# Layer B of a two-layer trunk: the results of the first four pairs of maps turned by VectorE and carried by transfers

## What is computed

```python
a = attn_map(q1b, k1) - lam * attn_map(q2b, k2)          # one pair of maps
o = einsum("bhqk,bhkd->bhqd", a, v)                      # 8 pairs, 128 columns each
o = o * rsqrt(mean(square(o), -1) + SUBLN_EPS)           # the norm of each pair
o = o * b_subln_g[j] * (1.0 - lambda_init)
x = layer_norm(ALPHA * x + o.reshape(B, S, D) @ b_w_o[j], ...)
```

## Time and profile before

| | |
|---|---|
| median of 3 runs | 590.24 us |
| the profiled execution | 590.63 us, of which its span 588.8 us |
| TensorE (PE) busy | 578.4 us, 98% of the span |
| VectorE (DVE) busy | 450.8 us, 77% |
| ScalarE (ACT) busy | 333.2 us, 57% |
| GpSimd (POOL) busy | 50.8 us, 9% |
| layer B's mixer, last 60 us of it | 340 to 400 us of the span |

### The profile page before, as it was taken

How to read it: one execution, slowest core, us unless ns; L and a number is a source line. 1 busy time by engine, 2 the same in 40 slices (tenths; PEclk the granted TensorE clock), 3 DMA queues, 4 the chain that set the end, 5 groups by cost and what they waited for, 6 DMA issues and landing times.

```text
span 588.8 us, 7729 instructions
## 1 busy us (share of the span) xinstructions
PE 578.4 (98%) x2708; PEld 473.0 (80%) x2708; DVE 450.8 (77%) x820; ACT 333.2 (57%) x557; POOL 50.8 (9%) x84
## 2 busy tenths in 40 slices
PE   8999999999999999999999999999999999999995
PEld 6887877888888888888888888888888888888884
DVE  4889996976688768767879796778677887766656
ACT  4767673345566656554545678945455565555530
POOL 5300000400000000000120003132000000000003
PEclk9999999999999999999999999999999999999998
DMA  8897876556768797866366965342965889767511
GB/s 302 296 325 227 277 220 173 195 181 206 223 205 267 251 350 231 261 235 202 143 212 216 300 183 173 132 144 72 314 186 178 254 260 339 247 228 244 179 36 71
DMA packets 96242, 128.65 MB, mean 218 GB/s; under 512 B 13468, under 2 KB 74188, under 8 KB 96204
## 3 DMA queue, kind: packets, MB, share of 16 engines
q1 hardware_dynamic: 94764, 123.97, 66.1%
q0 software_dynamic: 1152, 4.19, 2.0%
q10 hardware_dynamic: 288, 0.00, 0.0%
HBM read 108.23 MB, written 1.05 MB: 186 GB/s over the span
## 4 chain that ended last, share of the span: by engine, by line
PE 94%; DVE 2%; DMA 1%; SPq 1%; ACT 0%; issue 0%; DVEq 0%
PE wide L1305 17%; PE wide L1307 17%; PE wide L1306 17%; PE score L1307 6%; PE score L1306 6%; PE score L1305 6%; PE outb L1307 3%; PE turn L1307 3%; PE outb L1306 3%; PE turn L1306 3%; PE turn L1305 3%; PE outb L1305 3%; PE score L1321 1%; DMA xs<-in_x 1%; DMA spare<-turned 1%; PE wide L1400 1%
## 5 line engine op out<-in xcount | busy, mean ns | idle before, releaser
L988 DVE TENSOR_TENSOR w_lo<-raw,w_hi 128x2048 fp32r<-128x2048 f32 (+1 forms) x120 | 210.6, 1776 | 60.3 <-ACT w_hi L794 60.2
L794 ACT ACTIVATE w_hi<-raw 128x2048 fp32r<-128x2048 f32 (+1 forms) x126 | 184.1, 1488 | 101.5 <-PE wide L1307 48.2
L1305 PE MATMUL wide<-w_hi,oT_hi 128*128 128x512 f32 x240 | 94.7, 395 | 0.3 <-DVE oT_lo L1195 0.3
L1307 PE MATMUL wide<-w_hi,oT_lo 128*128 128x512 f32 x240 | 93.5, 390 | 0.0
L1306 PE MATMUL wide<-w_lo,oT_hi 128*128 128x512 f32 x240 | 93.5, 389 | 0.0
L1305 PE MATMUL wide<-w_hi,xT 128*128 128x512 f32 x224 | 89.7, 401 | 0.5 <-DVE xT L1013 0.3
L1307 PE MATMUL wide<-w_hi,xT 128*128 128x512 f32 x224 | 87.4, 390 | 0.0
L1306 PE MATMUL wide<-w_lo,xT 128*128 128x512 f32 x224 | 87.3, 390 | 0.0
L1305 PE MATMUL score<-w_hi,xT 128*128 128x512 f32 x160 | 62.2, 389 | 0.0
L1306 PE MATMUL score<-w_lo,xT 128*128 128x512 f32 x160 | 62.2, 389 | 0.0
L1307 PE MATMUL score<-w_hi,xT 128*128 128x512 f32 x160 | 62.2, 389 | 0.0
(11 more groups left out here) (164 smaller groups left out, 835.6 us busy)
## 6 DMA issues: line engine op xcount, KB each, us to landing
raw<-in_ffn_w_in SPq DMA_DIRECT2D x88, 512.0 KB, 5.4
raw<-in_ffn_w_out SPq DMA_DIRECT2D x22, 1024.0 KB, 7.5
kT<-turned SPq DMA_DIRECT2D x104, 128.0 KB, 2.8
raw<-in_a_w_qkv SPq DMA_DIRECT2D x9, 1024.0 KB, 6.9
raw<-in_w_kv_shared SPq DMA_DIRECT2D x8, 1024.0 KB, 5.9
raw<-in_a_w_o SPq DMA_DIRECT2D x4, 1024.0 KB, 6.0
raw<-in_b_w_q SPq DMA_DIRECT2D x4, 1024.0 KB, 5.1
raw<-in_b_w_o SPq DMA_DIRECT2D x4, 1024.0 KB, 5.4
```

What stands on the lines that cost most here:

```text
L794: ins = nc.scalar.activation(w_hi[c % RING][:, part], raw[c % RAW_RING][:, part], ACT.Copy)
L988: ins = nc.vector.tensor_tensor(w_lo[c % RING][:, part], raw[c % RAW_RING][:, part], w_hi[c % RING][:, part].bitcast(F32), ALU.subtract)
L1305: nc.tensor.matmul(dst, a_hi, b_hi, start=start, stop=False, skip_group_check=True)
L1307: return nc.tensor.matmul(dst, a_lo, b_hi, start=False, stop=stop, skip_group_check=True)
```

## The change

For the pairs 0 to 3 (`EARLY = 4`) `outT`, `out_hi` and `out_lo` of each pair are dropped. In their place:
- `out_turn` k (VectorE): one block transpose of `head_out` into the tile `turned`, after `subln` k; `subln` k+1 waits for it instead of for the TensorE transpose.
- `out_move` 0 (SP), once for the four pairs: a wait for the fourth turn, then four transfers of 128 KB from `turned` to `qk_rows`.
- `out_hi` 0 (ScalarE): four activations of 128x256, for all four pairs, from `qk_rows`; `out_lo` 0 (VectorE): eight operations of 128x128. The planner is told that they take 1.6 and 2.3 us, and that `out_hi` 0 comes behind `exp` 13 and `out_lo` 0 behind `norm` 6.
- every `wo` with kt of 0 to 3 needs `out_lo` 0.

`squares`, the scratch output of `square`, gets a second buffer. Pairs 4 to 7 are as before.

```diff
+    "out_turn": ("DVE", 0.45),
+    "out_move": ("SP", 3.0),
...
-LAG = {"move": 3.0, "prob_move": 3.0}
+LAG = {"move": 3.0, "prob_move": 3.0, "out_move": 3.0}
+EARLY = 4
...
-            add(("subln", k), ("mean", k), ("outT", k - 1))
-            add(("outT", k), ("subln", k))
-            add(("out_hi", k), ("outT", k))
-            add(("out_lo", k), ("out_hi", k))
+            add(("subln", k), ("mean", k), ("outT", k - 1), ("out_turn", k - 1))
+            if k < EARLY:
+                add(("out_turn", k), ("subln", k), *[("move", column(mat, 1)) for mat in range(2)])
+            else:
+                add(("outT", k), ("subln", k))
+                add(("out_hi", k), ("outT", k))
+                add(("out_lo", k), ("out_hi", k))
+            if k == EARLY - 1:
+                add(("out_move", 0), ("out_turn", k))
+                add(("out_hi", 0), ("out_move", 0))
+                add(("out_lo", 0), ("out_hi", 0))
+            if k == 6 and m == 13:
+                after[("out_hi", 0)].append(("exp", 13))
+                after[("out_lo", 0)].append(("norm", 6))
...
-                after[("wo", kt, st, half)].append(("out_lo", kt // 2 if A else kt))
+                after[("wo", kt, st, half)].append(("out_lo", kt // 2 if A else kt if kt >= EARLY else 0))
...
+        elif not A and step in (("out_hi", 0), ("out_lo", 0)):
+            takes = {"out_hi": 1.6, "out_lo": 2.3}[step[0]]
...
+            def out_move():
+
+                sp.wait_ge(early_turned_done, EARLY)
+                for a in range(4):
+                    sp.dma_start(early_moved[:, a * EARLY * 64:(a + 1) * EARLY * 64],
+                                 early_turned[32 * a:32 * a + 32].rearrange("p b k s j -> p b (k s j)")).then_inc(early_carried, 16)
...
+                    elif kind == "out_hi" and m < EARLY:
+                        act.wait_ge(early_carried, 64)
+                        for k in range(EARLY):
+                            last = nc.scalar.activation(oT_hi[:, k, :].rearrange("p (s a j) -> p s a j", s=ST, a=4), early_rows(k),
+                                                        ACT.Copy, scale=sub_gain[:, 0:1])
+                        last.then_inc(ohi_done, 1)
...
+                    elif kind == "out_turn":
+                        if m == 0:
+                            for mat in range(2):
+                                dve.wait_ge(moved[mat, 1], 128)
+                        dve.wait_ge(head_done, m + 1)
+                        nc.vector.transpose(early_turned[:, :, m].rearrange("p b s j -> p s b j"),
+                                            head_out.rearrange("p s (i b) -> p s b i", b=4)).then_inc(early_turned_done, 1)
+                    elif kind == "out_lo" and layer == 1 and m < EARLY:
+                        dve.wait_ge(ohi_done, SETS + 1)
+                        for k in range(EARLY):
+                            for st in range(ST):
+                                tokens = slice(st * P, (st + 1) * P)
+                                last = nc.vector.scalar_tensor_tensor(
+                                    oT_lo[:, k, tokens].rearrange("p (a j) -> p a j", a=4), early_rows(k)[:, st],
+                                    sub_gain[:, 0:1], oT_hi[:, k, tokens].bitcast(F32).rearrange("p (a j) -> p a j", a=4),
+                                    ALU.mult, ALU.subtract)
+                        last.then_inc(olo_done, 1)
...
+                            elif kt < EARLY:
+                                pe.wait_ge(olo_done, SETS + 1)
```

More of the change, by code:

```diff
@@ L296, in mixer_schedule @@
             turn_bank_free = None
-        elif step[0] in ("qkT_out", "probT_out") or not A and step[0] == "out_lo":
+        elif step[0] in ("qkT_out", "probT_out") or not A and step[0] == "out_lo" and step[1] >= EARLY:
             turn_bank_free = end[step]
@@ L440, in yoco_trunk @@
         head_out = spare[:, 2 * SEQ:3 * SEQ].rearrange("p (s d) -> p s d", s=ST)
-        squares = spare[:, 3 * SEQ:4 * SEQ].rearrange("p (s d) -> p s d", s=ST)
+        squares = spare[:, 3 * SEQ:5 * SEQ].rearrange("p (n s d) -> p n s d", n=2, s=ST)
         mean_sq = sb("mean_sq", [P, 2, ST])
@@ L454, in yoco_trunk @@
         prob_stage = [prob_stage[n].rearrange("p (b s k q) -> p b s k q", b=4, s=BATCH, k=3) for n in (0, 1, 2, 1)]
+        early_turned = turned[:, :, :, :].rearrange("p n b q -> p (n b q)")[:, 0:EARLY * SEQ].rearrange(
+            "p (b k s j) -> p b k s j", b=4, k=EARLY, s=ST)
+        early_moved = qk_rows[:, 0:EARLY * SEQ]
         conv_rows = sb("conv_rows", [4 * FT, LAYERS, P])
@@ L519, in yoco_trunk @@
         ohi_done, olo_done = sem("ohi_done"), sem("olo_done")
+        early_turned_done, early_carried = sem("early_turned_done"), sem("early_carried")
         y_done, var_done, std_done, norm_x_done = sem("y_done"), sem("var_done"), sem("std_done"), sem("norm_x_done")
@@ L533, in carried, with early_rows @@
             return in_moved.rearrange("p a (j s t) -> p j s a t", j=4, s=ST)[:, part]
+        def early_rows(k):
+            return early_moved.rearrange("p (a k s j) -> p k s a j", a=4, k=EARLY, s=ST)[:, k]
         def by_quarters(tile):
@@ L597, in load @@
                         move(layer, n)
+                    elif kind == "out_move":
+                        out_move()
                     else:
@@ L884, in _ @@
                         for st in range(ST):
-                            last = nc.scalar.activation(squares[:, st, :], head_rows[:, m % 2, st * P:(st + 1) * P],
+                            last = nc.scalar.activation(squares[:, m % 2, st, :], head_rows[:, m % 2, st * P:(st + 1) * P],
                                                         ACT.Square, accum_out=mean_sq[:, m % 2, st:st + 1])
@@ L1185, in _ @@
                         dve.wait_ge(rms_done, m + 1)
-                        if m >= 1:
+                        if m > EARLY:
                             dve.wait_ge(turn_filled, fill_of[(1, "outT", m - 1)] + 1)
+                        elif m:
+                            dve.wait_ge(early_turned_done, m)
                         for st in range(ST):
@@ L1191, in _ @@
                         last.then_inc(head_done, 1)
+                    elif kind == "out_turn":
[15 more added lines that the diff above has]
+                        last.then_inc(olo_done, 1)
                     elif kind == "out_lo":
-                        dve.wait_ge(ohi_done, SETS * layer + m + 1)
+                        dve.wait_ge(ohi_done, m + 1 if layer == 0 else SETS + 2 + m - EARLY)
                         if layer == 0:
```

## The result

The changed kernel has a median of 595.27 us (594.49 to 596.55, 4 runs), the kernel before 590.16 us in the same comparison. The ratio is 1.0088, 95% interval 1.0076 to 1.0101: **5.1 us slower**. I had said 592.6 with a range to 595.1, so the direction was right and the size was half of what came.

What follows compares the result with a forecast made beforehand. TensorE, busy 98% of the span, was taken as the bound. The profiled 590.63 us, less 0.9 for transposes, plus 3.3 idle, gave 593.0, or 592.6 for the median (+2.4); range 590.3 to 595.1.

Steps and rivals of the forecast that it cites:

- The gain: TensorE, four pairs of transposes removed: 0.225 us a pair by the starts, 0.9 us saved in all.
- The rival of dearer transposes: TensorE: the removed transposes save 2.2 us instead of 0.9, giving 591.3 us; chance 0.03.
- The mechanism: TensorE idles about 3.3 us before the first `wo`, nothing behind gives it back; `pv_out` 4, not the transfer, is late.
- Step 1: VectorE: `norm` 4 goes ahead of `subln` 3, put at 367.3; `out_turn` 3 takes 0.45 us and ends at 368.3.
- Step 2: `out_move` on SP: last issue at 370.3, landing 2.7 us after issue at 373.0, at worst 376.8.
- Step 3: ScalarE: `out_hi` 0 stands behind `drain` (5, 1), `exp` 14 and `pv_out` 4, which ends at 374.7, later than the transfer by 1.7.
- Steps 4 and 5: `out_hi` 0 on ScalarE takes 1.5 us, `out_lo` 0 on VectorE 1.95; `wo` starts at about 378.3.
- step 6: TensorE from 372.6 to 378.3: 5.7 us with 2.34 us of other work, so about 3.3 us idle.
- The clock: TensorE in the gap, busy 2.3 of 5.7 us: clock stays 1.00; its fall shared a rival's chance of 0.10.
- My rival of a late landing or a lower clock: Transfers meet the norm rows, or TensorE's clock falls: +4 to +6, 594.2 to 596.2 us; chance 0.10.
- The rival that ended on the other side, hidden: At the first `wo`, TensorE has enough other work until the rows are split: 589.3 to 590.2 us; chance 0.08.

Runs made afterwards that it cites:

- e4: The kernel before, with the two transposes of each of the eight pairs made four times: 595.45 us, 5.29 above the kernel before.
- e8: The changed kernel without the four transfers, `out_hi` 0 and `out_lo` 0 reading `turned` directly: 595.79 us, ratio 1.0095.
- e1: The changed kernel with a planner rule that puts the split of chunk 64 behind `out_hi` 0 and `out_lo` 0: 593.79 us, ratio 1.0065.
- e2: The changed kernel, its order kept, with 17 matmuls whose result nobody reads put into TensorE's gap: 594.11 us, ratio 1.0063.
- e3: The changed kernel with chunk 64's split behind `out_hi` 0 and `out_lo` 0, and 13 unread matmuls in TensorE's gap: 592.79 us, ratio 1.0046.
- e7: The change in two sets of two pairs, in the kernel before's order with urgent VectorE steps moved ahead and `out_hi` 1 behind `pv_out` 4: 589.57 us, ratio 0.9989.

## Why the prediction was right in direction and wrong in size

**The gain** was sized right: 0.225 us a pair from the starts, 0.22 by e4. The rival of dearer transposes is out; 24 pairs at 0.55 us would have given 603.4.

**The mechanism** was right: TensorE idles at the first `wo`, nothing behind it gives that back (the earlier trace rows and the last stretch shown above: 140.00 of 140.00 busy), and the transfer isn't the late member (e8). It becomes that only in e1, by 0.29 us.

**Step 1.** The hand-worked order held: `norm` 4 goes ahead of `subln` 3, which starts at 366.82. The turn was too cheap: I bounded a 128x256 turn by 0.40 and 0.57, and it took 0.64. It fell outside the rows that I called nearest; its layout isn't theirs, but no run shows that this is the reason. It moved nothing that is waited for.

**Step 2.** Landing 3.2 to 3.7 behind issue instead of 2.7, and up to 5.0 in e1 and e2: hidden in the changed kernel and in e2, 0.29 us visible in e1. The same four transfers in the same place thus varied by over 1 us from one profile to the next.

**Step 3 failed.** I listed `drain` (5, 1), `exp` 14 and `pv_out` 4 ahead of `out_hi` 0 and passed over the split of chunk 64. It is ready as soon as the last product of chunk 60 is done, that is with the same matmul that releases the drain, so the planner could start it right behind the drain, before `mask` 14 allowed `exp` 14, and it always takes what can start first. The weight of 7 us that holds this split back only decides among steps that can start together. `exp` 14 then came behind `out_hi` 0, at 378.11, and not ahead of it. Two us on ScalarE and 2.3 on VectorE stood in the chain's way and held it up by 0.75 (`pv_out` 4, ready at 374.3, starts at 375.03) and by 0.45 (`out_lo` 0): 1.2 us in the gap. The runs give 1.3 in the medians from e2 to e3, and 1.5 from the changed kernel to e1, where the clock is mixed in. The planner knew of it: in its own times, which `mixer_schedule` gives when it is executed, the first `wo` of the changed kernel stands 7.3 us behind the end of the last projection, and with e1's rule 6.4; the traces have 7.25 and 6.5.

**Steps 4 and 5** were undersized by 0.4 together: the four activations take 1.7 instead of 1.5, the eight operations 2.18 instead of 1.95. The guess that activations from SBUF would be shorter did not hold either: 0.50 us each, against 0.47 for `out_hi` 3. The 0.4 agree with the estimated 6.1 of e3 against the 5.7 of step 6; in e1 the late landing puts another 0.4 on top.

**The clock failed by the choice of a row.** I had it as a rival with 0.10, and took 98 to 100 us, 1.07 of 2 us busy at full clock, as the nearest row. That was a single gap between full stretches. Here three stretches of 2 us stand in a row at 1.27, 1.24 and 0.76 busy, and the clock fell in the third; in e8, as busy, in the fourth. My 2.3 of 5.7 us was as low as that from the start; I had read the level of one stretch and not that the gap goes on. e2 shows its price by itself: 1.2 us in the median, 2.0 in the profiled execution. The Trainium skill (TensorE: Matmul & The Clock Gate, HAM oscillation) warns of a TensorE that waits between short bursts of work, and then starts each burst at the lower clock. The rows at 376 to 384 agree with that, although here the longest wait in the gap was only 1.24 us.

In sum: +2.4 predicted, +0.2 more in e3 (+2.6, with 0.4 in its gap from its own fills), +1.3 for the order (e3 to e2), +1.2 for the clock (e2 to the changed kernel) make +5.1. These are differences between medians of three or four runs, so each is uncertain by some tenths; in the gaps of the traces steps 4 and 5 and the order can be seen by themselves, as 0.4 and 1.2.

My rival of a late landing or a lower clock had +4 to +6, which holds the measured +5.1, but by luck: the landing cost nothing, the clock 1.2, and without the order of step 3 the sum would have been 3.8.

The rival that ended on the other side, hidden, was not impossible in itself, only not in the orders tried here with one set of four: e7 is that case (its 0.55 below the kernel before, not the full 0.9), with a chain half as long for the first `wo` and eight products between the two sets.

## What to carry to other kernels

Work that is taken from the bound engine and gathered into one chain saves its own few tenths only if something covers the chain; ask first what the bound engine has to do while the chain runs, and cut the chain into pieces that are needed one after the other, as e7 does. When a greedy order is worked, list for each engine every step that can start at that moment, the background work above all: it fills each short wait of an urgent step with a long instruction. Better still, execute the planner and read its times, which here had the whole gap. And price an idle gap on TensorE twice, once for the time and once for the clock behind it, where the gap goes on for some us even if no single wait in it is long.

## What the runs showed of the hardware that I had not expected

- The granted clock went to 0.50 although TensorE was never idle for more than 1.24 us at a stretch: it had been busy 1.27, 1.24 and 0.76 of 2 us. It was back at 0.97 in the stretch 384 to 386, after 4 us of full work at the lower level. With nearly the same gap the clock fell about 2 us later in the profiles of e1 and e8 (0.88 and 0.92 in the stretch 378 to 380) and was on its way back in 382 to 384 (0.77 and 0.73). Against e2, whose clock stays up, the changed kernel lost between 0.4 and 2.4 us from run to run.
- A block transpose of 128x256 on VectorE took 0.64 us, longer than one of 128x384 (0.57) and nearly as long as one of 128x512 between other tiles of this kernel (0.69). Which stride does it, if it is one, was not looked into.

```profile
L1237 DVE STREAM_TRANSPOSE turned<-spare x4: 635/640/654, 361.6 to 367.3; 128x256 f32<-128x256 f32 x4
```

The row is the changed kernel's tile `turned`; the 0.69 is the median of the same tile's 128x512 transposes from `qk_rows`.
